# Broadcasting the decay sums of a state space recurrence by matmuls on four 32-row groups of the array, in three PSUM banks

## The reference, cut to what matters

```
acs   = cumsum(dt * a)                          # decay sums, one column for each head
L     = exp(acs[i] - acs[j]) for i >= j, else 0 # a 128x128 matrix for each head
y     = ((C @ B^T) * L) @ (dt * x) + exp(acs) * (C @ h)
h_new = exp(acs[last]) * h + (exp(acs[last] - acs) * B)^T @ (dt * x)
```

## Time and profile before

| | us |
|---|---|
| median of 3 runs | 3028.51 (3023.01 to 3032.23) |
| profiled execution, its own time | 3026.03 |
| its span | 3024.1 |
| TensorE busy | 2883.1 (95%) |
| VectorE busy | 1027.5 (34%) |
| ScalarE busy | 542.4 (18%) |
| GpSimd busy | 186.7 (6%) |

### The profile page before, as it was taken

One profiled execution on the slowest core, in us unless ns is written; L12 is line 12 of the kernel. 1 busy time (PEld: TensorE's weight loads), 2 busy tenths in 40 slices (PEclk: granted clock), 3 DMA queues, 4 the chain that ended last, 5 costly groups with the idle time before them and its releaser, 6 DMA issues.

```text
span 3024.1 us, 34166 instructions
## 1 busy us (share of the span) xinstructions
PE 2883.1 (95%) x13982; PEld 1403.5 (46%) x13983; DVE 1027.5 (34%) x1903; ACT 542.4 (18%) x1026; POOL 186.7 (6%) x281
## 2 busy tenths in 40 slices
PE   7899999999999999999979999998999998999998
PEld 3544354454444444444435545545545443444444
DVE  5841253233333333333343357344134222222101
ACT  3303321100110001010032133323133201000001
POOL 4200010000000000000000023000000000000000
PEclk9999989999999999999989999999999999999999
DMA  6146479999999999999973200200200231221210
GB/s 224 41 136 255 132 257 374 389 399 382 345 383 377 384 380 382 370 379 381 383 263 116 79 1 28 77 28 29 70 28 15 72 137 56 84 84 53 79 49 28
DMA packets 197306, 584.42 MB, mean 193 GB/s; under 512 B 15085, under 2 KB 23716, under 8 KB 197124
## 3 DMA queue, kind: packets, MB, share of 16 engines
q1 hardware_dynamic: 191744, 567.18, 49.9%
q0 software_dynamic: 4736, 14.88, 1.7%
q10 hardware_dynamic: 676, 0.21, 0.0%
HBM read 575.95 MB, written 4.19 MB: 192 GB/s over the span
## 4 chain that ended last, share of the span: by engine, by line
PE 85%; DVE 4%; issue 2%; ACT 1%; DMA 1%; PEld 0%; PEldq 0%; DVEq 0%; ACTq 0%
PE psum_all L213 82%; PE psum_all L221 3%; DMA panels<-in_ada_w 1%; DVE scratch L3872 1%; DVE hidden L2530 1%; PEld psum_all L213 0%; DVE scratch L3271 0%; DVE scratch L1993 0%; DVE hidden L4159 0%; DVE scratch L3888 0%; DVE scratch L1679 0%; ACT hidden L451 0%; DVE panels L3271 0%; ACT scratch L428 0%; DVE resid L1683 0%
## 5 line engine op out<-in xcount | busy, mean ns | idle before, releaser
L213 PE MATMUL psum_all<-panels,scratch 128*64 128x512 f32 (+4 forms) x6104 | 923.7, 479 | 10.7 <-issue 8.3
L213 PE MATMUL psum_all<-hidden,panels 128*128 128x512 f32 (+2 forms) x1792 | 798.3, 602 | 17.9 <-ACT hidden L451 15.3
L213 PEld LDWEIGHTS psum_all<-panels,scratch 128*64 128x64 f32 (+2 forms) x6104 | 365.6, 130 | 504.8 <-issue 438.3
L213 PEld LDWEIGHTS psum_all<-hidden,panels 128*128 128x128 f32 (+2 forms) x1792 | 335.5, 191 | 436.1 <-issue 415.5
L213 PE MATMUL psum_all<-scratch,panels 128*128 128x512 f32 (+2 forms) x816 | 308.5, 541 | 4.7 <-DVEq L4051 1.7
L213 PEld LDWEIGHTS psum_all<-scratch,panels 128*128 128x128 f32 (+1 forms) x816 | 153.2, 190 | 161.8 <-issue 149.4
L2530 DVE TENSOR_TENSOR hidden<-hidden,psum_all 128x512 f32<-128x512 f32 x264 | 164.4, 682 | 71.1 <-PE psum_all L213 70.7
L213 PE MATMUL psum_all<-scratch 128*64 128x128 f32 (+9 forms) x1284 | 164.7, 353 | 23.0 <-DVEq L3890 8.6
L213 PEld LDWEIGHTS psum_all<-scratch 128*64 128x64 f32 (+3 forms) x1284 | 110.2, 168 | 86.8 <-issue 60.3
L221 PE MATMUL psum_all<-const,scratch 128*128 128x128 f32 (+4 forms) x886 | 123.6, 270 | 22.2 <-DMA scratch<-in_c_ctx 8.0
L2238 ACT ACTIVATE scratch<-psum_all 128x512 f32<-128x512 f32 (+1 forms) x49 | 25.9, 528 | 601.7 <-PE psum_all L221 601.7
(11 more groups left out here) (347 smaller groups left out, 2104.6 us busy)
## 6 DMA issues: line engine op xcount, KB each, us to landing
panels<-in_exp_w_gu SPq DMA_DIRECT2D x132, 2048.0 KB, 13.0
panels<-in_exp_w_down SPq DMA_DIRECT2D x66, 2048.0 KB, 12.0
panels<-in_w_in SPq DMA_DIRECT2D x17, 2048.0 KB, 8.2
panels<-in_w_mod SPq DMA_DIRECT2D x11, 2048.0 KB, 7.8
panels<-in_ada_w SPq DMA_DIRECT2D x14, 1024.0 KB, 7.0
panels<-in_ada_w SPq DMA_DIRECT2D x5, 2048.0 KB, 20.7
panels<-in_ffn_w_gate SPq DMA_DIRECT2D x5, 2048.0 KB, 7.7
panels<-in_ffn_w_up SPq DMA_DIRECT2D x5, 2048.0 KB, 7.7
```

Source lines behind the costliest of these rows:

```text
L213: ins = self.pe.matmul(out, lhsT, rhs, start=start, stop=stop)
```

## The change

Each of the four matmuls reads 32 rows in place of 128. For this the rows are ordered so that those of q4 lie in rows 32\*q4 to 32\*q4+31: within them by direction, chunk and head of the group. VectorE's copy into `acs_own` does this reordering, one instruction for each direction. The weights are then 32x128 and the moving operand 32x512, in four different row groups of the array, and the four still write to the three banks in turn. The number of matmuls, their waits and their semaphores stay.

```
-        row_group, row_place, acs_own = part(SSM_TMP + 5120, 32), part(SSM_TMP + 5152, 4), part(SSM_TMP + 5156, 2, 64)
+        row_group, row_place, acs_own = part(SSM_TMP + 5120, 32), part(SSM_TMP + 5152, 4), part(SSM_TMP + 5156, P)
...
             for q4 in range(4):
                 pe.wait_ge(ssm_act.free, ssm_act.room())
                 bank = ssm_act.fill()
-                group = 16 * d + 4 * c + q4
-                mm(bank[:, :], row_group[:, group:group + 1].broadcast_to([P, P]), acs_rows).then_inc(ssm_act.full, 1)
+                strip, group = slice(32 * q4, 32 * q4 + 32), 8 * q4 + 4 * d + c
+                mm(bank[:, :], row_group[strip, group:group + 1].broadcast_to([32, P]), acs_rows[strip, :]).then_inc(ssm_act.full, 1)
...
-            mm.transpose(bank[:, 0:P], acs_own.rearrange("p d n -> p (d n)"), ident).then_inc(to_dve.full, 1)
+            mm.transpose(bank[:, 0:P], acs_own, ident).then_inc(to_dve.full, 1)
...
         def dve_acs_rows(dve, step):
-            dve.tensor_copy(acs_own, acs[:, :, 0:64]).then_inc(dve_done, 1)
+            for d in range(2):
+                dve.tensor_copy(acs_own.rearrange("p (q d c j) -> p d c q j", q=4, d=2, c=TT)[:, d],
+                                acs[:, d, 0:64].rearrange("p (c q j) -> p c q j", c=TT, q=4)).then_inc(dve_done, 1)
...
-            dve.wait_ge(dve_done, step.next(3))
+            dve.wait_ge(dve_done, step.next(4))
```

## The result

The changed kernel takes 3033.01 us (median of 18 runs, 3024.98 to 3038.43), the kernel before on the same chips 3025.66 us (18 runs, 3022.15 to 3032.23). The ratio is 1.0022, with a 95% interval of 1.0015 to 1.0029: slower by about 7 us, which is less than the 0.3% that was set ahead as the bound of "the same". The profiled execution took 3032.37 us (span 3030.6 and 1.8 around it), against 3026.0 before.

A forecast was written before the change was run, and what follows sets the result against it. In the recurrence PE's stream of matmuls was taken as the bound. Terms +1.7 + 0 + 0.1 + 6.8 = +8.6 on 3026.0 gave 3034.6, or 3037.1 on the median 3028.5; between them 3036, range 3025 to 3048.

The forecast's parts named there:

- forecast A: Recurrence: the bank wait takes the overlap back and the clock falls in about half the units, +5 to +12 us; chance 0.55.
- Overlap, then the bank wait: Seven warm units: three decay matmuls overlap, the fourth waits for a bank; 3.67 against 3.43 us a unit, +1.7 in all.
- rival E: Decay sums: the matmuls don't overlap, each waiting for a bank and a switch; +3 us, 3031; chance 0.05.
- First unit, 0: First unit of the recurrence: about 0.45 us gained against a clock that may stay low; bounds -0.45 and +1.4, taken as 0.
- VectorE's copy, +0.1: Copy ahead of the transpose: two half copies cost between nothing and +0.23 us more than one; taken as 0.1.
- The clock, 4 falls of 1.7, +6.8: Warm units: narrow work makes the clock fall in four of seven, 1.7 us each, +6.8; bounds 0 and +12 to +24.
- Rival B: Recurrence: the clock holds and only stalls, copy and first unit count; -0.5 to +3 us, 3029 to 3031; chance 0.25.
- Rival C: Decay sums: all four matmuls run side by side, 1.16 against 3.43 us a unit; -20 us in all, 3009; chance 0.05.

The follow-up runs named there:

- e4: Changed kernel plus one unused 128-row, 512-column matmul between third and fourth decay matmul of the seven later units: 3024.32 us, ratio 0.9988.
- e1: Changed kernel with the new row order and two copies kept, but the decay matmuls reading all 128 rows again: 3026.53 us, ratio 0.9998.
- e5: Changed kernel with all four decay matmuls on rows 0 to 31, so they run one after the other: 3032.18 us, ratio 1.0027.
- e8: Changed kernel plus one unused filler matmul reading 32 rows, between third and fourth decay matmul of the later units: 3029.59 us, ratio 1.0014.
- a2: The changed kernel profiled once more with nothing altered: 3034.16 us, a single run.
- a1: The changed kernel profiled and timed again with nothing altered: 3032.44 us, ratio 1.0027 to the kernel before.
- e3: Changed kernel with a fourth bank for the decay sums, taken from VectorE's ring in the recurrence: 3016.88 us, ratio 0.9955.
- e2: Changed kernel with the three z matmuls moved between the third and fourth decay matmul: 3020.17 us, ratio 0.9977.
- e7: Changed kernel plus two unused 128-row matmuls between third and fourth decay matmul of the later units: 3029.24 us, ratio 1.0011.
- e6: Changed kernel with a fourth bank for the decay sums, and three z passes moved ahead of the decay matmuls: 3013.94 us, ratio 0.9963.

## Why the prediction was right

It said 3036 us (3025 to 3048), "the same" most likely, slower next. Measured 3033.01, ratio 1.0022: forecast A held. The mechanism of the later units is the one that was forecast. The first unit's zero came about otherwise, and the number of falls was a guess that came near.

- **Overlap, then the bank wait.** Predicted: second pass at 0.62, Relu at 1.32, bank back at 2.51, z at 3.67, counted from the old start. Measured, with the start itself 0.09 later: 0.62, 1.31, 2.51, 3.56, and 0.10 more on the first z pass, 3.66. The +0.24 a unit (+1.7) was 0.21 (+1.5) in e4, where it stands alone. Bound "no overlap" (rival E) is refuted by the first row of the unit: six passes in 1.13 us.
- **First unit, 0.** The number was right, in part by luck. The two terms that were named don't cancel: 0.75 was gained at the state matmuls (0.45 forecast) and 1.52 lost by a clock that stayed low for 3 us more. What makes the sum zero is a term that the prediction didn't have, VectorE's product that takes 1.22 us beside no work of GpSimd and took 2.09 beside it.
- **VectorE's copy, +0.1.** Two copies take 0.30 us, where one took 0.23, so +0.07. The intervals of the totals, e1's too, are too wide to show it.

```profile
1731.08 0.30 DVE L3257 COPY scratch<-scratch 128x64 f32<-128x64 f32 x2
```

- **The clock, 4 falls of 1.7, +6.8.** Four in the first profile (8.19 - 1.47 = 6.7), three in each of the two others (5.1). Four was taken without a rule that gives it, between none and seven. Its reason, "not only when PE idles, but also after busy stretches of narrow work", is what e5 and e8 against e4 show. Its evidence was thinner than it looks: in the stretch at 196.84 there is a second wait, of 0.45 us, so PE idled there too, and it doesn't mention a fall behind busy full-height work (the row at 282.18, below). Rival B (the clock holds) is what e4 is in this stage: +1.5, as B priced it. Which of the units will be followed by a fall isn't explained; that e8 has them where the changed kernel has, and a2 where a1 has, suggests that where a unit stands in the execution counts, and not only what is in it.
- **The sum.** +8.6 forecast; the profiled execution is 6.3 above that of before, the stage in it 8.2. The rest of its span is 1.7 shorter, which is within what profiles of one kernel differ by: a1 and a2 have 1.2 and 1.8 us more than it behind the stage. On the medians it is +7.4. The 3036 stood on a base that was too high: the median of three was 3028.5, that of 18 is 3025.66, and 8.6 on that would be 3034.3.
- **Rival C (faster, 3009)** needed a bank to be free when the fourth matmul comes. e3 gave it one and came to 3016.88, 9.9 below its own before, where C had 20: the condition was named rightly, the price was too high. About half of the difference is VectorE, for which PE waits 4.8 us in the later units.
- **The band.** The changed kernel's runs lie 13 us apart (3024.98 to 3038.43), before's 10 (3022.15 to 3032.23): a number of falls that varies from run to run would do that. It was seen to vary in three profiles (4, 3, 3); that it makes the spread is argued, not shown.

## What to carry to other kernels

Before packing matmuls into row groups, count the banks for all that run at once: with one too few, the matmul that waits held all that stood behind it in PE's order, and the overlap of 1.6 us was worth less than nothing, while the same matmuls with independent work put between (e2, -6.6 us) or a fourth bank (e3, -10.5 us) gained. When the path ahead of a wait gets shorter, look for what stands behind it in the same queue and doesn't need it; move that up. And where PE is the bound, count how many of the array's rows the new work uses and look at the granted clock of the stretch, since 3.4 us at half the clock cost as much as eight units' stalls.

## What the runs showed of the hardware that wasn't expected

- The clock fell behind 3.69 us of 32-row matmuls without any pause (e5), and a gap of 1.28 us, closed to 0.44 with narrow work, changed nothing (e8, four falls); closed with full-height work it took all falls away (e4, e7). So in these units the rows in use counted. They aren't the only condition: e6's one fall is behind an idle time of 1.68 us among full-height matmuls, and the kernel before has a fall behind matmuls on all rows, nearly all of them with 1 or 128 columns, without a pause (the clock is 0.50 in the 3.4 us behind these rows):

```profile
282.18:285.57 3.39, 3.39 (x30) 3.20 (x29) 1.44 (x2) 1.07 (x3) 0.00 (x0) 1.00 1.03 412
282.78 2.84 PE L213 MATMUL psum_all<-scratch 128*128 128x128 f32 x22
```

- Two separate pieces of narrow work in a unit with 2.84 us of full-height matmuls between them (e2) had no fall in seven units; nor had four side by side for 1.07 us (e3), and none was behind them with z in front (e6).
- One change of shape costs 0.09 to 0.10 us at the start and 0.10 more on the first pass, whose weight load starts with it (both at 1778.33 in the changed unit above): first pass 0.53, the next 0.43, on entry and on exit (0.05 more in place of 0.10 where 64-column passes follow).
- Left open: why e4's total is 4.5 us below what I expected. From the end of the stage to the end of the span its profile has 1124.9 us (3023.16 - 1898.25), that of before 1129.3 (3024.11 - 1894.81). The ten other profiles fall into the same two groups: e5, e7 and e8 have 1124.4 to 1124.8, the changed kernel, a1, a2, e1, e2, e3 and e6 1127.8 to 1131.1. The largest part of it (2.5 us) lies at the start of grid attention, which is the same code in all: the clock is low there for 10 us in all eight profiles of the long group, and for 3.4 us in e4, e5, e7 and e8. A second such place follows near 2540, with 10 us against 6.8. At the first there are two idle times of PE, 2.40 and 2.29 us, in every profile; in the long group the clock falls at the first of them, in the short one only at the second. First the kernel before, then e4:

```profile
2210.80:2220.80 10.00, 7.68 (x14) 2.88 (x15) 4.30 (x7) 1.11 (x3) 0.00 (x0) 0.50 0.01 2
```

```profile
2216.00:2219.20 3.20, 2.90 (x9) 1.23 (x9) 0.19 (x1) 0.00 (x0) 0.00 (x0) 0.50 0.02 5
```

The time at which the stage ends doesn't sort the groups (short after 1898.25 and 1904.27, long after 1900.49 and 1902.82). Why a change in the recurrence should decide this 300 us later isn't known, and no run was made on it. If it holds in the timed runs too, the totals of e4, e5, e7 and e8 have it in them, which is why the argument above rests on the stage.
